# Meta rows of two attention branches: one product for a pair of heads, and one product over 80 stacked rows

## The reference

```python
# first branch: 8 heads, two scores each, values 128 wide, dense causal over meta + real keys
p = softmax(q @ k.T * scale + bias)            # for c = 0, 1
a = p[:, :, 0] - lam * p[:, :, 1]
ya = rmsnorm(a @ v, sub_g) * (1.0 - lam_init)
# second branch: 16 query heads over 2 key/value heads of width 64, window of 128,
# always-visible meta keys, and one sink per head
p = softmax(concat([s_meta, s_band, sink]))
o = einsum('bnqhgm,bmhd->bnqhgd', p_meta, vm) + einsum('bnqhgk,bnkhd->bnqhgd', p_band, vb)
mix = sigmoid(ga) * (ya @ w_branch_a) + sigmoid(gb) * (yb @ w_branch_b)
h = h + rmsnorm(mix @ w_out)
h = h + rmsnorm(square(relu(rmsnorm(h) @ w_ff1)) @ w_ff2)
```

## Time and profile before

| what | value |
|---|---|
| time, median of 3 runs | 1336.65 us (1336.33 to 1336.7) |
| profiled execution: its own time | 1336.75 us |
| its span | 1334.9 us |
| PE busy | 1327.2 us (99%) |
| PEld busy | 1133.4 us (85%) |
| DVE busy | 797.6 us (60%) |
| ACT busy | 629.3 us (47%) |
| POOL busy | 51.0 us (4%) |
| granted clock of TensorE, mean | 0.999 |

### The profile page before, as it was taken

The page is one execution under the profiler, slowest core; times in us unless marked ns, Lnnn a source line. Parts: engine busy times, 40 slices in busy tenths (PEclk is TensorE's granted clock), DMA queues, the critical chain, the costliest instruction groups (busy, mean ns, idle before and its releaser), DMA issues.

```text
span 1334.9 us, 19036 instructions
## 1 busy us (share of the span) xinstructions
PE 1327.2 (99%) x7118; PEld 1133.4 (85%) x7118; DVE 797.6 (60%) x1097; ACT 629.3 (47%) x912; POOL 51.0 (4%) x93
## 2 busy tenths in 40 slices
PE   9999999999999999999999999999999999999998
PEld 7889889888888888889988888888888888888886
DVE  6865565687875555557765555565556555556554
ACT  7554454455664443444644344443344444344442
POOL 1222110000000000000000000000000000000000
PEclk9999999999999999999999999999999999999999
DMA  9766555555566666774766666666666666666663
GB/s 313 202 184 168 159 157 161 161 159 152 168 191 189 189 189 213 228 239 156 251 189 191 190 194 188 190 192 197 191 190 189 189 193 196 194 188 189 190 191 109
DMA packets 147879, 252.55 MB, mean 189 GB/s; under 512 B 8659, under 2 KB 45935, under 8 KB 147420
## 3 DMA queue, kind: packets, MB, share of 16 engines
q1 hardware_dynamic: 143888, 241.40, 60.1%
q0 software_dynamic: 2160, 4.74, 1.9%
q10 hardware_dynamic: 1756, 5.36, 1.2%
HBM read 249.29 MB, written 2.17 MB: 188 GB/s over the span
## 4 chain that ended last, share of the span: by engine, by line
PE 98%; DMA 1%; ACT 0%; DVE 0%; issue 0%; ACTq 0%; SPq 0%
PE bank L1349 18%; PE bank L1351 17%; PE bank L1350 17%; PE bank L1661 16%; PE bank L1664 9%; PE bank L1395 4%; PE bank L1382 3%; PE bank L1383 3%; PE bank L1384 3%; PE bank L1397 2%; PE bank L1685 1%; DMA raw<-in_w_in 1%; PE bank L1688 1%; PE bank L1476 1%; PE bank L1475 1%; PE bank L1337 1%
## 5 line engine op out<-in xcount | busy, mean ns | idle before, releaser
L811 DVE TENSOR_TENSOR w_lo<-raw,w_hi 128x1024 fp32r<-128x1024 f32 (+1 forms) x456 | 549.9, 1214 | 435.7 <-ACT w_hi L437 433.8
L437 ACT ACTIVATE w_hi<-raw 128x1024 fp32r<-128x1024 f32 (+1 forms) x456 | 474.2, 1049 | 486.9 <-DMA raw<-in_w_ff 361.5
L1661 PE MATMUL bank<-f_hl,w_hi 128*128 128x512 f32 x960 | 229.7, 391 | 0.0
L1661 PEld LDWEIGHTS bank<-f_hl,w_hi 128*128 128x128 f32 x960 | 176.4, 188 | 34.1
L1349 PE MATMUL bank<-w_hi,hid_hi 128*128 128x512 f32 x512 | 199.2, 389 | 0.0
L1350 PE MATMUL bank<-w_lo,hid_hi 128*128 128x512 f32 x512 | 199.2, 389 | 0.0
L1351 PE MATMUL bank<-w_hi,hid_lo 128*128 128x512 f32 x512 | 199.2, 389 | 0.0
L1664 PEld LDWEIGHTS bank<-f_hl,w_lo 128*128 128x128 f32 x960 | 123.1, 191 | 4.7
L1664 PE MATMUL bank<-f_hl,w_lo 128*128 128x256 f32 x960 | 124.5, 283 | 0.0
L1349 PEld LDWEIGHTS bank<-w_hi,hid_hi 128*128 128x128 f32 x512 | 96.1, 188 | 20.0
L1351 PEld LDWEIGHTS bank<-w_hi,hid_lo 128*128 128x128 f32 x512 | 96.1, 188 | 20.0
(11 more groups left out here) (246 smaller groups left out, 1510.0 us busy)
## 6 DMA issues: line engine op xcount, KB each, us to landing
raw<-in_w_ff SPq DMA_DIRECT2D x256, 512.0 KB, 3.8
raw<-in_w_in SPq DMA_DIRECT2D x128, 512.0 KB, 3.8
raw<-in_w_out SPq DMA_DIRECT2D x32, 512.0 KB, 4.5
raw<-in_w_branch_b SPq DMA_DIRECT2D x16, 512.0 KB, 3.9
raw<-in_w_branch_a SPq DMA_DIRECT2D x16, 512.0 KB, 3.8
xt<-in_turned_x SPq DMA_DIRECT2D x8, 272.0 KB, 5.2
raw<-in_w_in SPq DMA_DIRECT2D x8, 256.0 KB, 5.3
bias<-bias_table POOLq DMA_DIRECT2D x8, 256.0 KB, 4.6
```

The source lines that it names most:

```text
L437: act.activation(w_hi[:, u, :, 0:width], raw[:, u, :, 0:width], ACT.Copy).then_inc(hi_ready, 1)
L811: dve.tensor_tensor(w_lo[:, u, :, 0:width], raw[:, u, :, 0:width], w_hi[:, u, :, 0:width].bitcast(F32), ALU.subtract).then_inc(lo_ready, 1)
L1661: ins = pe.matmul(acc[g][:], w_hi[:, u, k, cols], f_hl[:, kt, :], start=kt == 0, stop=kt == KT - 1)
```

## The change

**Second branch.** The probabilities of a pair for the 16 meta keys are copied side by side (`t_meta`, 32 columns: head 0, head 1) and transposed together, once for each block of 128 queries. The meta values of each group are kept twice in `vb_m`, as 32 rows by 128 columns: rows 0 to 15 hold the values in the columns of head 0 and zeros in those of head 1, rows 16 to 31 the other way round (a mask of ones and zeros, `head_mask`). One product of 32 rows by 128 columns then takes the place of two of 16 rows by 64 columns.

**First branch.** The meta probabilities are copied five times side by side (`t_stack`, 80 columns for each block) and transposed to 80 rows. Values and probabilities are laid over these rows so that one product gives high by high (rows 0 to 15), low by high (rows 32 to 47) and high by low (rows 64 to 79); the rows between are zeroed on the side of the values by `part_mask`. One product takes the place of three, and its only wait is for `pTm_kept`.

```diff
-        pT_hi, pT_lo, pTm_hi, pTm_lo = pTr[:, 0, :], pTr[:, 1, :], pTmr[0:META, 0, :], pTmr[0:META, 1, :]
+STACK = 5 * META
+AT_LO, AT_P_LO = slice(2 * META, 3 * META), slice(4 * META, 5 * META)
+        t_meta = pTm[:, 1, 0:4 * META].rearrange("p (q n) -> p q n", q=2)
+        t_stack = pTm[:, 1, 0:2 * STACK].rearrange("p (q n) -> p q n", q=2)
+        v_stack = flat[:, 2 * KEYS:2 * KEYS + 2 * STACK].rearrange("p (d n) -> p d n", d=2)
...
@@ gpsimd
-            pool.memset(pTmr[:].bitcast(F32), 0.0)
-            pool.memset(vam_lo0[:].bitcast(F32), 0.0).then_inc(meta_zero, 1)
             for j in range(JOBS):
-                if j == HB // 2:
-                    pool.wait_ge(max_ready, j)
-                    pool.memset(vam_lo2[:].bitcast(F32), 0.0).then_inc(meta_zero, 1)
                 job_bias(j)
+                if j == HB // 2 + 1:
+                    pool.wait_ge(o_ready, HB // 2)
+                    pool.memset(pTmr[:].bitcast(F32), 0.0).then_inc(pad_zero, 1)
@@ scalar, job_keep_probs
-                    act.activation(over_two(pTm_hi), meta_probs(), ACT.Copy).then_inc(pTm_hi_ready, 1)
+                    act.wait_ge(pad_zero, 1)
+                    act.activation(pTmr[0:STACK, :], S1[0:STACK, 0:2 * P], ACT.Copy).then_inc(pTm_hi_ready, 1)
                     return
+                act.activation(pTm[0:2 * META, 0, 0:P], TB[0:2 * META, 3 * P:4 * P], ACT.Copy)
                 for e, src in enumerate((TB, S0)):
-                    act.activation(pTm[:, e, 0:P], src[0:META, 3 * P:4 * P], ACT.Copy)
                     last = act.activation(pT[:, e, :], src[:, 0:3 * P], ACT.Copy)
@@ vector, once: masks before keep_roots, one copy in keep_scales, vb_m by two masked copies
+            def mask_heads():
+                link(dve.tensor_reduce(head_mask, ident[0:2 * META, 0:2 * META].rearrange("p (e k) -> p e k", e=2), AX.X,
+                                       ALU.add))
+            def mask_parts():
+                parts = ident[0:STACK, 0:STACK].rearrange("p (i k) -> p i k", i=5)
+                link(dve.tensor_reduce(part_mask, parts[:, ::2, :], AX.XY, ALU.add))
@@ vector, scale_values (4 times)
+                link(last)
+                dve.tensor_copy(v_stack.rearrange("p d (i k) -> p d i k", i=5), five(v_s[:, :, SEQ:KEYS])).then_inc(va_scaled, 1)
@@ vector, job_combine: pairs, then first branch
+                    link(last)
+                    for q, a in ((0, 1), (1, n0 + 1)):
+                        last = dve.tensor_copy(t_meta[:, q, :].rearrange("p (e k) -> p e k", e=2), t[:, :, a:a + META])
                     last.then_inc(probs_ready, 1)
                     return
...
-                last.then_inc(probs_ready, 1)
+                link(last)
+                dve.tensor_copy(t_stack.rearrange("p q (i k) -> p q i k", i=5),
+                                five(t[:, 0, 0:2 * n0].rearrange("p (q c) -> p q c", q=2)[:, :, 0:META]))                   .then_inc(probs_ready, 1)
@@ tensor, job_turn
-                    pe.transpose((dst[0:META, 3 * P:4 * P] if windowed else S1[0:META, 0:P]), t[:, e, s0:r0], ident[:])
-                    m1 = S1[0:META, e * P:(e + 1) * P] if windowed else S1[0:META, P:2 * P]
-                    ins = pe.transpose(m1, t[:, e, n0 + s0:n0 + r0], ident[:])
+                    if not windowed:
+                        pe.transpose(S1[0:STACK, 0:P], t_stack[:, 0, :], ident[:])
+                        ins = pe.transpose(S1[0:STACK, P:2 * P], t_stack[:, 1, :], ident[:])
+                if windowed:
+                    pe.transpose(TB[0:2 * META, 3 * P:4 * P], t_meta[:, 0, :], ident[:])
+                    ins = pe.transpose(S1[0:2 * META, 0:P], t_meta[:, 1, :], ident[:])
@@ tensor, job_values: pairs, then first branch
-                    for e in range(2):
-                        pe.matmul(o[e], vb_m[:, col], pTm[:, e, :], start=True, stop=False)
+                    pe.matmul(MB[:, 0:2 * P], vb_m[:, j // 4, :], pTm[0:2 * META, 0, :], start=True, stop=False)
...
-                pe.wait_ge(pTm_hi_ready, h + 1)
-                pe.matmul(o, va_m[:, col], pTm_all[0], start=False, stop=False)
-                pe.matmul(o, vml, pTm_all[0], start=False, stop=False)
                 pe.wait_ge(pTm_kept, j + 1)
-                pe.matmul(o, va_m[:, col], pTm_all[1], start=False, stop=False)
+                pe.matmul(o, va_m[:, col], pTmr[:], start=False, stop=False)
```

More of the change, by code:

```diff
@@ L174, in hybrid_block @@
             [("yA", [P, HA, SEQ], F32), ("yT", [P, HB // 2, SEQ], F32), ("t", [P, 2, 418], F32), ("pT", [P, 2, 3 * P], F32),
-             ("pTm", [META, 2, 2 * P], F32), ("bias", [P, 2, 2, 418], F32)],
+             ("pTm", [P, 2, 2 * P], F32), ("bias", [P, 2, 2, 418], F32)],
             [("gap2", [P, HA, SEQ], F32), ("gap3", [P, HB // 2, SEQ], F32), ("gap4", [P, 2, 418], F32),
-             ("pTr", [P, 2, 3 * P], F32R), ("pTmr", [P, 2, 2 * P], F32R)],
+             ("pTr", [P, 2, 3 * P], F32R), ("pTmr", [P, 2 * P], F32R)],
             [("gap7", [P, 7884], F32), ("sq_hi", [P, SEQ], F32R)],
@@ L312, in over_two, with five @@
             return v.rearrange("p (q t) -> p q t", q=2)
-        def meta_probs():
-            return S1[0:META, 0:2 * P].rearrange("p (s t) -> p s t", t=P)
+        def five(v):
+            return v.rearrange("p d (i k) -> p d i k", i=1).broadcast_to([P, 2, 5, META])
         block = ctx.enter_context(nc.Block())
@@ L874, in keep_scales @@
                 dve.wait_ge(acc_free, 2)
[L875 removed]
+                link(dve.tensor_tensor(kv_s, kv_s, both(rstd_bc[:]), ALU.mult))
+                dve.tensor_copy(kv_meta.rearrange("p (e k) -> p e k", e=2), both(kv_s[:, 1, SEQ:KEYS])).then_inc(kv_ready, 1)
             def both(v):
@@ L960, in keep_turned @@
                     dve.tensor_copy(vb[:], TB[:, 0:SEQ].rearrange("p (b n) -> p b n", b=BLOCKS))
-                    last = dve.tensor_copy(vb_m[:], TB[0:META, SEQ:SEQ + P])
+                    both_groups = TB[0:2 * META, SEQ:SEQ + P].rearrange("p (g n) -> p g n", g=HKV)
+                    for e in range(2):
+                        last = dve.tensor_scalar(vb_m[:, :, e * DHB:(e + 1) * DHB], both_groups, head_mask[:, e:e + 1],
+                                                 None, ALU.mult)
                 last.then_inc(proj_kept, 1)
@@ L1414, in turn_scales @@
                 pe.transpose(S0[:, SEQ:KEYS], rstd_t[0:META, 2, :], ident[0:META, 0:META]).then_inc(scales_turned, 1)
-            def turn_heads(bank_of, src, d):
-                for b in range(BLOCKS):
-                    pe.transpose(bank_of[:, b * P:(b + 1) * P], src[:, d, b * P:(b + 1) * P], ident[:])
-                return pe.transpose(bank_of[0:META, SEQ:SEQ + P], src[:, d, SEQ:KEYS], ident[:])
             def turn_values(i, h):
                 c = TURNED_VALUES[i]
-                pe.wait_ge(va_scaled, 2 * (2 * i + h + 1))
+                pe.wait_ge(va_scaled, 2 * i + h + 1)
                 for d, ps in enumerate(acc_of(c, h)):
-                    ins = turn_heads(ps, v_s, d)
+                    for b in range(BLOCKS):
+                        pe.transpose(ps[:, b * P:(b + 1) * P], v_s[:, d, b * P:(b + 1) * P], ident[:])
+                    ins = pe.transpose(ps[0:STACK, SEQ:SEQ + P], v_stack[:, d, :], ident[:])
                 ins.then_inc(va_turned, 1)
@@ L1445, in turn_rows @@
                                       start=True, stop=True)
-                    turn_heads(TB, kv_s, 1).then_inc(proj_turned, 1)
+                    for b in range(BLOCKS):
+                        pe.transpose(TB[:, b * P:(b + 1) * P], kv_s[:, 1, b * P:(b + 1) * P], ident[:])
+                    pe.transpose(TB[0:2 * META, SEQ:SEQ + P], kv_meta, ident[:]).then_inc(proj_turned, 1)
                     return
```

39 lines of the change are left out of this document (21 added, 18 removed).

## The result

The changed kernel takes 1339.3 us (median of 16 runs, 1338.8 to 1340.05) against 1336.3 before (16 runs, 1335.86 to 1337.12): ratio 1.0023, 95% interval 1.0016 to 1.0029. It is slower by 3.0 us, and outside the range of the forecast.

The account below looks back on a forecast made before the run. PE was taken as the bound (98% of the chain), except jobs 10 to 15, set by DVE and ACT. -1.76 + 0.4 - 0.2 + 1.7 = +0.14 us gave 1336.8 us, range 1334.6 to 1338.2.

Parts of the forecast that it names:

- Transposes and product of a pair: Second branch on PE: two meta transposes per pair instead of four, -1.76 us; the merged product's wider weight load, +0.4 us.
- DVE and ACT form a ring of their own: First branch, jobs 10 to 15: DVE and ACT set a 13.99 us period; DVE work added between maxima is paid fully.
- The copy: DVE's 128x160 copy into the first branch's stack, with its link: 0.27 us a job, +1.7 us in all.
- In job 8 DVE waits 0.63 us for ACT at L1017, and the copies ... are covered: First branch, job 8: the wait hides the copies of combination and values, together some 0.55 us, so job 8 pays nothing.
- shortens nothing that PE waits for: Second branch: on ACT and DVE one copy per pair is gone or shorter, counted as no gain.
- Products of the first branch: On PE one product replaces three, 0.23 us less per job, counting only behind job 15's last wait at L1489: -0.2 us.
- PE alone counts: Rival: the ring has unseen slack, so all 8 first-branch jobs give their 0.23; -3.2 us, 1333.5 us; chance 0.13.
- The copy stalls: Rival: DVE's stack copy is held up, 0.75 us a job, +3.5 us, 1340.1 us; chance 0.10, shared with another such wait.
- another wait of that size in the ring: Rival sharing the stalling copy's 0.10 chance: some other wait of that size appears in the DVE and ACT ring; slower.
- A slip in the bounds: Bounds of DVE's stack copy, 0.20 and 0.36 us a job, were said to give totals of 1336.4 and 1337.3 us.

Follow-up runs that it names:

- `second_only`: Only the second branch's edits (a pair's meta rows in one product, two transposes instead of four) on the kernel before, first branch unchanged; 1334.84 us, ratio 0.998 to 0.9998.
- `before_plus_copy`: The kernel before with only a link and a 128x160 DVE copy added after a first-branch head's combination, into a tile nobody reads; 1338.07 us, ratio 1.0005 to 1.0023.
- `v_low_at_zero`: The changed kernel with the low parts' places exchanged: values' at partition 0 (L966), probabilities' at partition 32 (L1044); 1338.48 us, ratio 1.0007 to 1.0025.
- `first_only`: Only the first branch's edits on the kernel before, the pairs of the second branch unchanged; 1340.48 us, ratio 1.0018 to 1.0043.

## Why the prediction was wrong

- **Transposes and product of a pair (-1.76, +0.4): right.** 8 transposes at 0.11 and 0.63 us at the product; `second_only` gained 1.40 us between the marks.
- **"DVE and ACT form a ring of their own ... work added to DVE between maximum and maximum is paid in full": right for the copy, too simple as a rule.** The waits at the transposes grew with the copy, and moving one instruction out of the ring gave most of the time back. But DVE doesn't wait once in a period, as I read it: it also stands 0.12 us behind L1019 for ACT's `w_hi`. The copy was paid because it lies ahead of the transposes, where this second wait begins; the late start of L1044, between the transposes and the wait's end, was not.
- **The copy, 0.27 a job, +1.7 in all: right in size** (0.28; +1.67 measured alone).
- **The step that failed is the one behind it: the copy was taken as all that the change adds to the ring.** L1044 (before L1019) and L966 (before L949) were costed at nothing, since their kind and length are the same. They had moved to partitions 64 and 32, and DVE instructions behind them started late. From the scores of job 8 to the transposes of job 15 the loss over the forecast was 4.13 - 1.7 = 2.4: 5 x 0.22 in jobs 10 to 14, 0.28 in job 9 (0.34 instead of 0.06) and 1.07 in job 8. The 0.22 a job are almost all L1056's late start and longer copy, an effect of L1044. Job 8's is 0.22 for L1044, 0.56 for L966 and 0.27 for ACT. L1422, waiting for L966, adds 0.34 ahead of job 8. From the first scores to the end the traces have 4.13 - 1.05 - 0.29 = +2.79, where the forecast had +0.14.
- **"In job 8 DVE waits 0.63 us for ACT at L1017, and the copies ... are covered": right, but the wait's end was taken as fixed.** Of the wait's 0.63, 0.55 for the copies would leave 0.08; 0.34 are left, since the wait's end comes 0.27 later, most of it by ACT's longer copies. Those I had costed at nothing as well ("shortens nothing that PE waits for" looked at pairs alone). In `before_plus_copy` one copy took the wait to 0.35 and the job stayed at 14.46. With 14.95 in `v_low_at_zero` the rest of job 8 is 0.27 + 0.22.
- **Products of the first branch, -0.2 (job 15 only): right.** From the transposes of job 15 to the first product with `y_hi` it is 24.02 us before, 23.74 after and 23.79 in `first_only`, but 23.98 in `second_only`, which keeps the three products. (To the very end the changed kernel is 0.29 shorter, and `second_only` 0.19, so that difference alone would show nothing.) With the ring open each job gives its 0.22.
- **The rivals.** "PE alone counts", 1333.5, was wrong for the change and is close to what the changed kernel takes with the ring open: 1333.2 to 1334.3. "The copy stalls" named a result close by, 1340.1, and the wrong mechanism: the copy takes its 0.24. The "another wait of that size in the ring" that I gave a tenth was nearest to the case, though it named no instruction.
- **A slip in the bounds.** With 0.20 and 0.36 for the copy the sum gives 1336.3 and 1337.4, not 1336.4 and 1337.3. It changes nothing in the result.

What the runs don't separate is how the 0.12 of L1056 behind a reciprocal that reads no PSUM would fall if only L1044's output, or only its input, began at another partition. That was not tried, and neither was the masked copy on ACT by itself.

## What the runs showed of the hardware

A DVE instruction that begins at another partition than its forerunners doesn't overlap them. L1044 starts 0.57 us after L1042 at partition 64 or 32 and 0.47 at 0. The one behind it starts 0.03 after its end and not 0.07 to 0.08 before it, as L964 in job 8 shows, where ACT has no part in it. And one comes later: L1056, which reads PSUM, is 0.12 late (1.78 for 1.66), although a `w_lo` and a reciprocal, both within SBUF and at their usual spacing to each other, lie between. If an instruction that reads PSUM at partition 0 follows at once, as L964 in job 8 of `v_low_at_zero`, then the later L1056 is at its usual 1.13. Unoverlapped, the copy takes 0.42 instead of 0.36 us in job 11 (0.42 instead of 0.41 in job 8). Each such start comes 0.09 to 0.13 us later; whether that costs time depends on what waits next. In job 8 all are paid, in job 11 that of L1056 alone.

The Trainium skill has the rule: VectorE: DVE Perf Modes, "Two Vector instructions with no wait between them", says that an instruction starts only when all earlier ones have finished if its input from SBUF or from PSUM begins in another group of 32 partitions than the first input that the last instruction to read that memory took from it, and likewise for its output and the last one written there. By it L1044, the next instruction and the next reader of PSUM are held, which are the three of job 11, and in job 8 L1044, the L964 behind it, both L966, the L964 between them, L815 and L1056, which are the seven seen to start behind the end of the one in front. The trace agrees in these ten places, L815 of job 11 with the proviso that ACT's `w_hi` ends there at the same time; the page gives no time for a hold, the rows do.

## What to carry to other kernels

When a change gives an instruction other partitions, read it as a new instruction, even where operation and shape stay: on DVE a low part that begins at partition 32 or 64 made itself and one or two later instructions start 0.1 us late each. In job 8 all of that was paid; in the jobs behind it only the last start was, 0.2 us with the longer copy, because the one before it waited for ACT in any case. Before work is saved on the engine that is busy 99% of the time, look for a second engine that is never waiting for it: here the first branch's saving came only when DVE's ring was opened by moving one 1.75 us instruction into a wait of 2.9 us, and that move made the work added in those jobs free as well. And work put ahead of a wait is covered only up to its end, which the same change can move: here by 0.27 us, mostly through a copy on ACT that had got a mask as its scale and five times the rows.
